# Dividing the taps of a causal convolution anew between GpSimd, VectorE and ScalarE, and holding weight parts in four places

## What is computed

```python
u = h @ w_pw1 + b_pw1                       # 1024 -> 2048
a, gate = jnp.split(u, 2, axis=-1)
u = a * jax.nn.sigmoid(gate)
u = jnp.pad(u, ((0, 0), (CONV_WIDTH - 1, 0), (0, 0)))          # CONV_WIDTH = 31
u = lax.conv_general_dilated(u, w_dw[:, None, :], window_strides=(1,), padding='VALID',
                             dimension_numbers=('NWC', 'WIO', 'NWC'),
                             feature_group_count=D_MODEL) + b_dw
u = jax.nn.silu(layer_norm(u, ln_g, ln_b))
return u @ w_pw2 + b_pw2
```

## Time and profile before

| | |
|---|---|
| median of 3 runs | 1959.86 us (1958.95 to 1960.28) |
| the profiled execution's own time | 1959.82 us |
| its span | 1957.9 us |
| TensorE busy | 1914.1 us, 98% of the span |
| DVE, ACT, POOL busy | 42%, 40%, 34% |

### The profile page before, as it was taken

One profiled execution on the slowest core, in us unless ns is written; L12 is line 12 of the kernel. 1 busy time (PEld: TensorE's weight loads), 2 busy tenths in 40 slices (PEclk: granted clock), 3 DMA queues, 4 the chain that ended last, 5 costly groups with the idle time before them and its releaser, 6 DMA issues.

```text
span 1957.9 us, 24867 instructions
## 1 busy us (share of the span) xinstructions
PE 1914.1 (98%) x9826; PEld 1594.8 (81%) x9826; DVE 827.4 (42%) x1368; ACT 775.7 (40%) x1164; POOL 670.8 (34%) x208
## 2 busy tenths in 40 slices
PE   6998999999999999999999999999999999999999
PEld 4665988888897779888888897778998898888887
DVE  5997721111266474612111387756552352122122
ACT  6565432222345462523222256754454342122221
POOL 2884044444401210243343312222123403434442
PEclk9999999999999999999999999999999999999999
DMA  5111263223221211322222312111122322222222
GB/s 191 65 43 66 69 128 94 108 86 107 86 92 45 86 44 46 107 107 89 105 107 86 108 55 87 65 49 60 44 71 102 111 85 107 97 97 88 106 82 91
DMA packets 30366, 169.40 MB, mean 87 GB/s; under 512 B 3739, under 2 KB 6076, under 8 KB 13372
## 3 DMA queue, kind: packets, MB, share of 16 engines
q1 hardware_dynamic: 30268, 168.01, 25.5%
HBM read 162.22 MB, written 5.77 MB: 86 GB/s over the span
## 4 chain that ended last, share of the span: by engine, by line
PE 89%; DVE 6%; ACT 3%; issue 1%; POOL 1%; DMA 0%; DVEq 0%; SPq 0%; POOLq 0%; ACTq 0%
PE ps L2083 62%; PE ps L2104 8%; PE ps L2440 4%; PE ps L2506 3%; PE ps L2195 1%; PE ps L2598 1%; PE ps L2166 1%; POOL wlo L515 1%; DVE ps L1426 1%; ACT whi L604 1%; PE ps L2616 1%; DVE wlo L1263 1%; PE ps L2329 1%; PE ps L2346 1%; PE ps L2347 1%
## 5 line engine op out<-in xcount | busy, mean ns | idle before, releaser
L515 POOL TENSOR_TENSOR wlo<-wraw,whi 128x2048 fp32r<-128x2048 f32 (+5 forms) x142 | 588.5, 4145 | 1260.7 <-ACT whi L604 1229.2
L604 ACT ACTIVATE whi<-wraw 128x2048 fp32r<-128x2048 f32 (+5 forms) x158 | 275.8, 1745 | 372.7 <-PE ps L2083 349.3
L2083 PE MATMUL ps<-xh,whi 128*128 128x512 f32 x1044 | 413.5, 396 | 4.8 <-DVE xl L1243 3.7
L2083 PE MATMUL ps<-xl,whi 128*128 128x512 f32 x1044 | 407.1, 390 | 0.0
L2083 PE MATMUL ps<-xh,wlo 128*128 128x512 f32 x1044 | 407.0, 390 | 0.0
L2083 PE MATMUL ps<-hh,whi 128*128 128x512 f32 x752 | 295.4, 393 | 5.9 <-DVE hl L1503 5.7
L2083 PE MATMUL ps<-hl,whi 128*128 128x512 f32 x752 | 293.4, 390 | 0.0
L2083 PE MATMUL ps<-hh,wlo 128*128 128x512 f32 x752 | 293.3, 390 | 0.0
L2083 PEld LDWEIGHTS ps<-xh,whi 128*128 128x128 f32 x1044 | 196.5, 188 | 50.5 <-issue 9.2
L2083 PEld LDWEIGHTS ps<-xl,whi 128*128 128x128 f32 x1044 | 196.5, 188 | 43.1 <-issue 3.1
L2083 PEld LDWEIGHTS ps<-xh,wlo 128*128 128x128 f32 x1044 | 196.4, 188 | 41.1
(11 more groups left out here) (333 smaller groups left out, 2820.9 us busy)
## 6 DMA issues: line engine op xcount, KB each, us to landing
wraw<-stream SPq DMA_DIRECT2D x132, 1024.0 KB, 4.8
wraw<-stream SPq DMA_DIRECT2D x12, 768.0 KB, 4.1
wraw<-stream SPq DMA_DIRECT2D x6, 384.0 KB, 3.3
resid<-x SPq DMA_DIRECT2D x4, 512.0 KB, 5.4
wraw<-stream SPq DMA_DIRECT2D x8, 256.0 KB, 3.0
branch_scratch<-RS SPq DMA_DIRECT2D x8, 256.0 KB, 2.0
wraw<-stream SPq DMA_DIRECT2D x4, 512.0 KB, 3.8
out<-resid SPq DMA_DIRECT2D x4, 512.0 KB, 2.8
```

What stands on the lines that cost most here:

```text
L515: pool.tensor_tensor(wlo[:, p, 0:w], wraw[:, p, 0:w], whi[:, p, 0:w], ALU.subtract).then_inc(lo_ready, 1)
L604: act.activation(whi[:, p, 0:w], wraw[:, p, 0:w], ACT.Copy).then_inc(hi_ready, 1)
L2083: ins = pe.matmul(ps[:, bank + n, :], wt[:, p, w], xt[:, k0 + k, :], start=k == 0 and q == 0, stop=k == k_tiles - 1 and q == 2)
```

## The change

GpSimd's share grows from seven to eight products in tiles 0 to 6 (`POOL_TAPS` 8; tile 7 keeps seven, `POOL_LAST`), and VectorE's shrinks from 20 to 19 taps there, ten in the even and nine in the odd chain. GpSimd's sum is no longer read by VectorE: ScalarE waits for it and copies it into the bank of the odd chain (`products_banked`), and the chain's first link reads the bank. In tile 7 it waits for the shifted sum. ScalarE's rounded part of a chunk is made one tile earlier, between the fourth and the fifth product; that of chunk 2 now stands ahead of the first sigmoid. To have room for it, the parts of chunks 2, 3, 6 and 7 are put into `hh` and `hl`, which are unused until the layer norm. ScalarE's and GpSimd's loops over tiles are written out.

```diff
-PE_TAPS, POOL_TAPS = 4, 7
+PE_TAPS, POOL_TAPS, POOL_LAST = 4, 8, 7
 
 DVE_TAPS = TAPS - PE_TAPS - POOL_TAPS
 LAST_TAPS = 5
-HALF_CHAIN = DVE_TAPS // 4
+EVENS, ODDS = (DVE_TAPS + 1) // 2, DVE_TAPS // 2
 NH, NOPE, ROPE, QKD = 8, 128, 64, 192
...
 
+        lent = tuple(t.rearrange("p t n -> p (t n)") for t in (hh[:, :, :], hl[:, :, :]))
+
+        def weights(c):
+
+            if c < DT and c // 2 % 2:
+                return lent[c % 2][:, 0:CW], lent[c % 2][:, CW:2 * CW]
+            return whi[:, c % 2, :], wlo[:, c % 2, :]
+
+        def weights_free(eng, c, h=0):
+
+            if c >= DT + 2:
+                eng.wait_ge(chunk_done, h * 2 + (c - 1))
+            elif c >= 4:
+                eng.wait_ge(chunk_done, c - 3)
+
...
                 p, w = c % 2, WIDTH[c]
+                hi, lo = weights(c)
                 pool.wait_ge(hi_ready, h * 2 + (c + 1))
-                if c >= 2:
-                    pool.wait_ge(chunk_done, h * 2 + (c - 1))
-                pool.tensor_tensor(wlo[:, p, 0:w], wraw[:, p, 0:w], whi[:, p, 0:w],
-                                   ALU.subtract).then_inc(lo_ready, 1)
-
-            def add_products(j, h=0):
-                for i in range(1, POOL_TAPS):
-                    pool.wait_ge(products_scaled, h * (2 * POOL_TAPS) + (j * POOL_TAPS + i + 1))
+                weights_free(pool, c, h)
+                pool.tensor_tensor(lo[:, 0:w], wraw[:, p, 0:w], hi[:, 0:w], ALU.subtract).then_inc(lo_ready, 1)
...
             pool.wait_ge(lo_ready, 2)
             rest(2)
-            add_products(0)
-            rest(3)
-            add_products(1)
-            with pool.Fori(1, DT // 2 - 1) as h:
-                for j in range(2):
-                    rest(2 + j, h)
-                    add_products(j, h)
+            for j in range(DT - 2):
+                add_products(j)
+                rest(3 + j)
...
-            rest(DT)
             add_products(DT - 2)
             pool.wait_ge(shift_ready, 1)
             for j in range(3):
                 shift(j)
-            add_products(DT - 1)
-            pool.wait_ge(products_added, DT * (POOL_TAPS - 1))
+            add_products(DT - 1, POOL_LAST)
+            pool.wait_ge(products_added, (DT - 1) * (POOL_TAPS - 1) + POOL_LAST - 1)
             pool.tensor_tensor(pool_sum[1], pool_sum[1], RS[:, :], ALU.subtract).then_inc(products_shifted, 1)
...
-                                   scale=tap(PE_TAPS + i, j, h)).then_inc(products_scaled, 1)
+                        act.wait_ge(products_added, j * (POOL_TAPS - 1) + max(1, i - 4))
+                    elif i == 0 and j:
+                        act.wait_ge(products_added, j * (POOL_TAPS - 1))
+                    act.activation(product[i], shifted(PE_TAPS + i, j), ACT.Copy,
+                                   scale=tap(PE_TAPS + i, j)).then_inc(products_scaled, 1)
+                    if i == 3 and j < DT - 1:
+                        head(c0 + j + 3)
...
-                act.activation(last_diag[i], ident, ACT.Copy, scale=tap(PE_TAPS + POOL_TAPS + i, 1, DT // 2 - 1))
-            sigmoid(0)
+                act.activation(last_diag[i], ident, ACT.Copy, scale=tap(PE_TAPS + POOL_LAST + i, DT - 1))
             head(c0 + 2)
-            conv_products(0)
-                if j:
+            for j in range(DT):
+                if j >= 2:
+                    tap_weights(j)
+                if j == DT - 1:
                     act.wait_ge(shift_summed, 1)
                     step(act.activation(ps[:, SHIFT, :], ps[:, SHIFT, :], ACT.Copy, scale=1.0 / P))
                     act.activation(RS[:, :], ps[:, SHIFT, :], ACT.Copy).then_inc(shift_ready, 1)
-                sigmoid(j, DT // 2 - 1)
-                head(c0 + j + DT)
-                conv_products(j, DT // 2 - 1)
+                sigmoid(j)
+                conv_products(j, POOL_LAST if j == DT - 1 else POOL_TAPS)
+                if j == DT - 1:
+                    act.wait_ge(products_shifted, 1)
+                else:
+                    act.wait_ge(products_added, (j + 1) * (POOL_TAPS - 1))
+                act.activation(ps[:, ODD_BANK[j % 2], :], pool_sum[j % 2], ACT.Copy).then_inc(products_banked, 1)
...
                 elif chain == 0:
                     dve.wait_ge(pe_taps_done, h * 2 + (j + 1))
-                elif shifted_sum:
-                    dve.wait_ge(products_shifted, 1)
-                    was = pool_sum[at].unsqueeze(1)
                 else:
-                    dve.wait_ge(products_added, h * (2 * POOL_TAPS - 2) + (j + 1) * (POOL_TAPS - 1))
-                    was = pool_sum[at].unsqueeze(1)
+                    dve.wait_ge(products_banked, h * 2 + (j + 1))
                 last = chain and m == taps - even - 1
-                dve.scalar_tensor_tensor(out=NT[:, at:at + 1, :] if last else acc, in0=x, scalar=tap(k, j, h), in1=was,
+                dve.scalar_tensor_tensor(out=NT[:, at:at + 1, :] if last else acc, in0=x, scalar=tap(k, j, h), in1=acc,
...
 
             def middle(j, h, n, first, last):
                 for m in range(first, last):
-                    tap_add(j, h, 1, m, n + (2 * m - 1))
-                    tap_add(j, h, 0, HALF_CHAIN + m, n + 2 * m)
+                    tap_add(j, h, 0, EVENS // 2 + m, n + max(2 * m - 1, 0))
+                    if m < ODDS - EVENS // 2:
+                        tap_add(j, h, 1, m, n + 2 * m)
...
```

More of the change, by code:

```diff
@@ L752, in conv_products @@
-            def conv_products(j, h=0):
-                gated(act, j, h)
-                for i in range(POOL_TAPS):
+                               bias=vec("b_pw1", DT + j)).then_inc(gate_ready, 1)
+            def conv_products(j, n=POOL_TAPS):
+                gated(act, j)
+                for i in range(n):
                     if i >= 4:
-                        act.wait_ge(products_added, h * (2 * POOL_TAPS - 2) +
-                                    (j * (POOL_TAPS - 1) + max(1, i - 4)))
-                    elif i == 0 and not (isinstance(h, int) and j == 0):
-                        act.wait_ge(products_added, h * (2 * POOL_TAPS - 2) + j * (POOL_TAPS - 1))
-                    src = shifted(PE_TAPS + i, j, h)
-                    act.activation(product[i].unsqueeze(1), src.unsqueeze(1) if isinstance(h, int) else src, ACT.Copy,
-                                   scale=tap(PE_TAPS + i, j, h)).then_inc(products_scaled, 1)
+                        act.wait_ge(products_added, j * (POOL_TAPS - 1) + max(1, i - 4))
[5 more added lines that the diff above has]
+                        head(c0 + j + 3)
@@ L1401, in gate, with tap_add @@
                                          in1=SQ[:, at:at + 1, :], op0=ALU.add, op1=ALU.mult).then_inc(pair_free[at], 1)
-            def tap_add(j, h, chain, m, done, taps=DVE_TAPS, shifted_sum=False):
+            def tap_add(j, h, chain, m, done, taps=DVE_TAPS):
                 at = j % 2
@@ L1413, in tap_add @@
                     x = x.unsqueeze(1)
-                was = acc
                 if m:
@@ L1463, in _ @@
                     end_and_begin(j, h, n)
-                    middle(j, h, n + 2 * HALF_CHAIN, 0, 1)
+                    middle(j, h, n + EVENS, 0, 1)
                     gate(j + 1, h)
-                    middle(j, h, n + 2 * HALF_CHAIN, 1, HALF_CHAIN)
-            j, h, left = 1, DT // 2 - 1, DVE_TAPS - LAST_TAPS
+                    middle(j, h, n + EVENS, 1, EVENS // 2)
+            j, h, left = 1, DT // 2 - 1, TAPS - PE_TAPS - POOL_LAST - LAST_TAPS
             n = begun + (DT - 2) * DVE_TAPS
-            for m in range(HALF_CHAIN):
-                tap_add(0, h, 1, HALF_CHAIN + m, n + m - (m == 0))
-            n += HALF_CHAIN
+            for m in range(EVENS // 2):
+                tap_add(0, h, 1, ODDS - EVENS // 2 + m, n + m - (m == 0))
+            n += EVENS // 2
             tile_sum(0, h, n)
@@ L1476, in _ @@
                 tap_add(1, h, 0, m + 1, n + max(2 * m, 1), left)
-                tap_add(1, h, 1, m, n + 2 * m + 1, left, True)
+                tap_add(1, h, 1, m, n + 2 * m + 1, left)
             tile_sum(1, h, n + left)
@@ L2081, in project @@
                     w = slice(k * 2 * P + n * P, k * 2 * P + (n + 1) * P)
-                    for q, (wt, xt) in enumerate(passes(hi, lo, whi, wlo)):
-                        ins = pe.matmul(ps[:, bank + n, :], wt[:, p, w], xt[:, k0 + k, :],
+                    for q, (wt, xt) in enumerate(passes(hi, lo, *weights(c))):
+                        ins = pe.matmul(ps[:, bank + n, :], wt[:, w], xt[:, k0 + k, :],
                                         start=k == 0 and q == 0, stop=k == k_tiles - 1 and q == 2)
@@ L2191, in taps @@
                     pe.wait_ge(conv_ready, 2 * h + j - 1)
-                weights = [(k, diag[at][k]) for k in range(PE_TAPS)]
-                weights += [(PE_TAPS + POOL_TAPS + i, last_diag[i]) for i in range(more)]
-                for n, (k, w) in enumerate(weights):
+                diags = [(k, diag[at][k]) for k in range(PE_TAPS)]
```

(4 more changed lines are left out.)

55 lines of the change are left out of this document (21 added, 34 removed).

## The result

The changed kernel takes 1967.39 us (median of 6 runs, 1964.98 to 1968.42) against 1960.07 beside it (6 runs, 1958.95 to 1960.78): 7.3 us slower, ratio 1.0036 with a 95% interval of 1.0026 to 1.0046. The forecast was 1965.4 in a range of 1961.5 to 1968.5, with 0.65 on slower. The profiled execution took 1965.77 (span 1963.8), 6.0 more than the one of before.

A forecast was written before the change was run, and what follows sets the result against it. VectorE was taken to set the convolution's pace at 14.98 us per tile, with TensorE busy 98% of the span. Later squares 3.8 plus clock 1.8 make 5.6 us on 1959.82, so 1965.4; range 1961.5 to 1968.5.

The forecast's parts named there:

- forecast case: Whole kernel: later squares and a fall of TensorE's clock add 5.6 us, giving 1965.4; chance 0.42.
- the loop: Per tile: sigmoid, gate, first product, GpSimd's additions, copy, diagonals, next sigmoid; 14.5 us from sigmoid to sigmoid.
- Part 1: VectorE's work: one tap less in seven tiles saves 4.6 us, the first odd link about 0.9 twice; 13.9 per tile left.
- Part 2: Middle tiles: the limit passes from VectorE at 14.98 to a ScalarE-GpSimd loop at 14.5; some 2.4 us gained.
- Part 3: Start: rounded part before sigmoid 0 costs 1.8 us, sigmoid 1 3.4 late; with the queue at the end, gate 7 1.3 later.
- Part 4: Last tile: GpSimd's shifts (3.7 us) wait for the later mean; VectorE's last sum starts 2.0 us later.
- Part 5: Squares: table load and squares wait behind the last copy; eleven matmul pairs (9.4 us) put tile 7's sum 3.8 us later.
- Part 6: TensorE's clock: falls in a 4.2 us idle before the squares, costing about 1.8 us; ends 0 and 3.
- rival 2: Squares in the tail: they hide, only VectorE's 2.0 us remain, 1961.8; chance 0.13.
- rival 3: Middle tiles: the loop never closes, TensorE sets the pace at 14.2, faster at 1956.1; chance 0.07.
- rival 1: TensorE's idle before the squares: the clock stays up, 1963.6; chance 0.25.
- Rival 4: Loop: slower than summed, each 0.3 us (a copy of 0.85) costs 2.1 us, 1967.5 to 1969; chance 0.13.

The follow-up runs named there:

- the repeat: The changed kernel itself measured and profiled once more, nothing altered: 1967.33 us, ratio 1.0039.
- two kernels that free them: Changed kernel with VectorE reading tile 7's shifted sum directly, no last copy: 1964.36 us; changed kernel with table load and two squares ahead of the last copy: 1963.81 us.
- both orders mended: Changed kernel with copy behind next sigmoid, gate before odd link, table and two squares early; in the variant cited VectorE reads tile 7's sum without a copy: 1960.44 us.
- seven products, table first: Changed kernel with seven products and 20 taps in all tiles, and table load and two squares ahead of the last copy: 1958.66 us, ratio 0.9994.

## Why the prediction was right, and where it was off

The forecast case is the one that happened, and 1967.39 lies inside the range, 2.0 above the point. That the first profiled execution (1965.77) lies only 0.4 from the point is luck: the loop and the queues took more than was summed, and the 1.8 us put down for the clock cost 0.1 there. By its parts:

| event | before | forecast | after |
|---|---|---|---|
| sigmoid 2 | 60.5 | 65.1 | 64.64 |
| sigmoid 6 | 120.3 | 123.1 | 124.03 |
| gate 7 | 138.22 | 139.5 | 140.81 |
| subtraction of the mean begins | 148.83 | 151.1 | 152.14 |
| table load | 143.86 | 153.0 | 154.06 |
| sum of tile 7 | 160.61 | 164.4 | 165.84 |

**Part 1** held: VectorE's work fell by 3.9 us in the five tiles and nothing of it showed.

**Part 2** held in its mechanism and missed in one term. Addition by addition and with the copy (0.54 to the next instruction, 0.55 said) the loop is as summed, but the gate stands 0.92 behind its sigmoid, not 0.71. That row was taken at gate 0, which lies outside VectorE's register loop. In the changed kernel gates 0 and 1 lie outside it (0.70, 0.71), and gates 2 to 7, inside it, take 0.92 to 0.94. So a pass is 14.76 for 14.5. That a register's value in the wait is the cause is argued, not shown. One of the four passes from sigmoid 2 to 6 took 15.10: GpSimd stood still for 0.48 us ahead of its last addition. In all that is 1.4 us on these four; sigmoid 2 had been 0.5 early, which leaves the 0.9 late at sigmoid 6. The queue of diagonals and means ahead of sigmoid 7 came as said.

**Part 3** was right about sigmoid 1 (49.08 for 49.5) and for the right reason only in half: the rounded part ahead of sigmoid 0 was priced as a loss of 1.8 us that nothing hides, and taking it away gained nothing. GpSimd's first seven additions are the whole of it.

**Part 4** held: three shifts took 3.73 (3.7 said), as with the two-operand link gone they should, and additions and subtraction went as summed, 1.0 late by what they inherited. VectorE's last sum was 2.96 later, not 2.0, and that is the same 1.0: it began 8.7 behind the end of the copy, as summed. In the profiled execution VectorE also waited 1.80 for nine taps of TensorE at the lower clock, but that cost nothing: in the repeat, with the taps at full clock, the last sum stands as far behind its copy (163.57 - 154.26 = 9.31, and 162.76 - 153.44 = 9.32).

**Part 5** held in its mechanism: the queue of squares ended the stretch, and two kernels that free them gain 3.0 and 3.6 us. That it is the costliest place is not shown: in their profiles the sum of tile 7 comes only 2.1 and 2.3 us earlier, of the 5.2 by which it was late, since the tail of part 4 lies beneath, and going back to seven products gains as much (4.2 us, 4.6 at the sum of tile 7). The eleven pairs took 165.84 - 156.13 = 9.7 us for 9.4.

**Part 6** priced the clock at 1.8 us with ends 0 and 3. Filling the idle stretches is worth 1.4 us by the medians; a profile at the median shows 1.5 and the first one 0.1. But the place was only half right: there is a second idle stretch, 3.09 us ahead of the taps of tile 7, that I did not look at (2.75 before, clock 1.00), and in the first profile the clock fell there. My reading that the fall comes with the longer idle failed: it held for the repeat, but the clock also fell behind idles of 1.83 and 2.00 us (the kernel with both orders mended in which VectorE reads the last sum, and the one with seven products: nine taps in 9.66 us each) and stayed up behind 3.10.

**Rivals.** The squares did not hide (rival 2), the loop closed (rival 3), and the clock did not stay up (rival 1). Rival 4, a longer pass, came in part and through another term than the copy. The forecast at 1965.4 misses that 0.25 per pass: 0.9 to 1.3 us by gate 7, and the 0.8 us behind the first product of `w_pw2`.

The single costs, as differences of medians, are 4.2 us for the eighth product, 3.6 for the last copy's place and 1.4 for the clock, together 9.2, where the change took 7.3. The first two add up within the noise: without both (seven products, table first) the kernel stands 1.3 us under before, where 7.3 - 7.8 would leave it 0.5 under, and the intervals are about 2 us either way. The clock is not a third cost beside them: in that kernel TensorE's idles are 2.01 us ahead of the taps and 0.41 within the squares, where the repeat had 3.10 and 3.95. No run takes the clock away by itself there, so its own share stays open.

## What to carry to other kernels

A wait placed in an in-order queue holds everything behind it: before an engine takes over a copy, write down what comes next in its queue and who waits for that, and look for a ring. Here the copy itself was 0.6 us, and the order around it cost 8.4, TensorE's clock included; with the copy behind the sigmoid, the gate ahead of the link that reads it, and the table ahead of the last copy, the same division of work costs nothing, and gains nothing that can be measured either. Taking work off the busiest engine gains only down to the next limit, here 14.3 us of TensorE's work per tile for a period of 14.98.
